# Bank order inside a group of 24 matmuls: one PSUM bank after the other instead of in turn

## What is computed

```
xn = rmsnorm(x)
u, v, q, k, va, ga, gb = split(xn @ w_in)
a  = gelu(u) * (tril(W_s) @ rmsnorm(gelu(v)) + bias)
b  = sliding_window_attention(q, k, va)
h  = sigmoid(ga) * (a @ w_oa) + sigmoid(gb) * (b @ w_ob)
x  = x + h @ w_out
x  = x + relu(rmsnorm(x) @ w_up)**2 @ w_down      # w_up 1024 x 4096
y  = rmsnorm(x)
```

## Time and profile before

| | |
|---|---|
| median of 3 runs | 1637.41 us (1636.24 to 1639.02) |
| profiled execution | 1637.21 us |
| its span, first to last instruction | 1635.5 us |
| PE busy | 1553.7 us, 95% |
| VectorE busy | 1053.4 us, 64% |
| ScalarE busy | 765.8 us, 47% |
| share of line 1538 (the matmuls of `product`) in the chain that ended last | 66.4% |
| mean granted TensorE clock | 0.977 |

### The profile page before, as it was taken

One profiled execution on the slowest core, in us unless ns is written; L12 is line 12 of the kernel. 1 busy time (PEld: TensorE's weight loads), 2 busy tenths in 40 slices (PEclk: granted clock), 3 DMA queues, 4 the chain that ended last, 5 costly groups with the idle time before them and its releaser, 6 DMA issues.

```text
span 1635.5 us, 28812 instructions
## 1 busy us (share of the span) xinstructions
PE 1553.7 (95%) x12226; PEld 1518.1 (93%) x12226; DVE 1053.4 (64%) x1377; ACT 765.8 (47%) x1159; POOL 181.7 (11%) x206
## 2 busy tenths in 40 slices
PE   3999999999998989999995999999999999999998
PEld 3988888889998989999995999999999999999997
DVE  3455554402766666766674776876687678767875
ACT  5465555522644544555441464533553355335533
POOL 4222322200000010000110040000000000000001
PEclk7999999999999999999997999999999999999999
DMA  7611110132859524545568343636363645454522
GB/s 244 195 29 27 29 29 21 35 116 78 206 162 279 156 50 106 152 107 155 130 176 218 112 115 89 170 94 165 104 155 110 149 119 140 124 135 128 132 63 104
DMA packets 105353, 200.64 MB, mean 123 GB/s; under 512 B 16592, under 2 KB 44240, under 8 KB 97896
## 3 DMA queue, kind: packets, MB, share of 16 engines
q1 hardware_dynamic: 88288, 127.64, 23.4%
q0 software_dynamic: 10384, 64.00, 20.1%
q10 hardware_dynamic: 6552, 7.13, 1.3%
HBM read 121.77 MB, written 19.30 MB: 86 GB/s over the span
## 4 chain that ended last, share of the span: by engine, by line
PE 82%; DMA 5%; DVE 5%; ACT 4%; issue 2%; SPq 2%; POOL 1%; ACTq 0%; DVEq 0%; POOLq 0%
PE ps L1538 66%; PE ps L1330 10%; PE ps L1318 2%; DMA res<-x_keep 2%; ACT prob L741 1%; PE ps L1376 1%; DVE prob L1006 1%; DMA xn<-xn_keep 1%; DMA raw<-in_w_in 1%; PE ps L1394 1%; POOL prob L559 1%; SPq L407 1%; DVE y_t L1307 1%; PE ps L1516 1%; DVE w_lo L956 1%
## 5 line engine op out<-in xcount | busy, mean ns | idle before, releaser
L1538 PE MATMUL ps<-xp_hi,wp_hi 128*128 128x258 f32 x3136 | 636.0, 284 | 23.6 <-DVE wp_lo L1110 18.9
L1538 PE MATMUL ps<-xp_lo,wp_hi 128*128 128x258 f32 x3136 | 637.0, 285 | 0.0
L1538 PE MATMUL ps<-xp_hi,wp_lo 128*128 128x258 f32 x3136 | 636.0, 285 | 0.0
L1538 PEld LDWEIGHTS ps<-xp_hi,wp_hi 128*128 128x128 f32 x3136 | 491.9, 191 | 24.7 <-DVE wp_lo L1110 19.5
L1538 PEld LDWEIGHTS ps<-xp_hi,wp_lo 128*128 128x128 f32 x3136 | 491.4, 191 | 0.0
L1538 PEld LDWEIGHTS ps<-xp_lo,wp_hi 128*128 128x128 f32 x3136 | 488.3, 191 | 0.0
L677 ACT ACTIVATE wp_hi<-wbuf 128x1024 fp32r<-128x1024 f32 x196 | 208.0, 1061 | 554.2 <-PE ps L1538 553.9
L1110 DVE TENSOR_TENSOR wp_lo<-wbuf,wp_hi 128x1024 fp32r<-128x1024 f32 x196 | 243.6, 1243 | 170.5 <-ACT wp_hi L677 170.5
L1330 PE MATMUL ps<-xn_hi,w_hi 128*128 128x344 f32 x480 | 159.7, 333 | 2.0 <-DVE q_st L986 2.0
L1330 PE MATMUL ps<-xn_lo,w_hi 128*128 128x344 f32 x480 | 155.1, 323 | 0.0
L1330 PE MATMUL ps<-xn_hi,w_lo 128*128 128x344 f32 x480 | 155.1, 323 | 0.0
(11 more groups left out here) (191 smaller groups left out, 1526.4 us busy)
## 6 DMA issues: line engine op xcount, KB each, us to landing
wbuf<-wbuf POOLq DMA_DIRECT2D x57, 1024.0 KB, 7.5
wbuf<-in_w_up SPq DMA_DIRECT2D x24, 1024.0 KB, 5.5
wbuf<-in_w_down SPq DMA_DIRECT2D x24, 1024.0 KB, 5.1
wbuf<-in_w_in SPq DMA_DIRECT2D x18, 1024.0 KB, 5.6
raw<-in_w_in SPq DMA_DIRECT2D x40, 256.0 KB, 3.4
wbuf<-in_w_ob SPq DMA_DIRECT2D x6, 1024.0 KB, 7.1
wbuf<-in_w_oa SPq DMA_DIRECT2D x6, 1024.0 KB, 5.2
wbuf<-in_w_out SPq DMA_DIRECT2D x6, 1024.0 KB, 5.4
```

Of the source, the lines that this page charges most:

```text
L1538: last = mm(ps[:, 2 * p + b, 0:HN], w[:, (2 * n + p // 2) % 2, k, p % 2 * P:(p % 2 + 1) * P], x[n % 2][:, k, b * HN:(b + 1) * HN], start=( ...
```

## The change

In `product` the loop over the two halves b moves from the innermost place to the outermost. Before, the 24 matmuls of a group alternate between the two banks, and two neighbours share their weights. After, twelve go to bank 2p and then twelve to bank 2p + 1; each weight tile is read for the first half and again twelve matmuls later for the second. The number of matmuls, weight loads and waits is the same, and so are the buffers and the flags for starting and ending an accumulation in each bank. The wait for the second part of `xp_split` stands before k = 2 of the first half, which is the 7th matmul of the group instead of the 13th. `prod_done` is still raised once, by the 24th.

```diff
-                for k in range(MH):
-                    if p == 0 and k % 2 == 0:
-                        pe.wait_ge(xp_split, 2 * n + k // 2 + 1)
-                    for m, (w, x) in enumerate(passes):
-                        for b in range(2):
+                for b in range(2):
+                    for k in range(MH):
+                        if p == 0 and b == 0 and k % 2 == 0:
+                            pe.wait_ge(xp_split, 2 * n + k // 2 + 1)
+                        for m, (w, x) in enumerate(passes):
                             last = mm(ps[:, 2 * p + b, 0:HN], w[:, (2 * n + p // 2) % 2, k, p % 2 * P:(p % 2 + 1) * P],
                                       x[n % 2][:, k, b * HN:(b + 1) * HN], start=(first and k == 0 and m == 0),
                                       stop=(k == MH - 1 and m == 2), skip_group_check=not first)
```

## The result

The changed kernel is faster: median 1626.89 us of 7 runs (1625.84 to 1632.23) against 1637.41 us of the kernel before (1634.7 to 1639.71, 7 runs), ratio 0.9942 with a 95% interval of 0.9927 to 0.9957. That is 10.5 us or 0.6% less. I had forecast no change, 1637.6 us, with a range of 1629 to 1648, and missed.

A forecast was written before the change was run, and what follows sets the result against it. PE bounds the kernel, with an unbroken run of matmuls 120.6 ns apart. Counts, reading out and distance at 0 plus 0.36 us for the wait, on 1637.21 us, gave 1637.6 us, range 1629 to 1648.

The forecast's parts named there:

- What bounds the kernel: PE, busy 95% of the span, with matmuls 120.6 ns apart from 1000 us on; 0.35 ns each makes 0.2%.
- The counts and the reading out: Matmul and weight load counts stay, and both banks are still read after the 24th matmul: 0 us each.
- The wait for the second half of x: Moved to the 7th matmul, it stops PE at g = 6 for i = 0 and i = 1: 0.07 + 0.29 us.
- the 0.36 us of the sum: Total of all forecast terms, made up of 0.07 + 0.29 us from the two new stops of PE at g = 6.
- The distance from start to start: Time between starts of neighbouring matmuls in a group, 120.5 ns before: claimed unchanged, 0 us, chance 0.48.
- bounds of +1.2 and -1.3: Limits in ns on the change per matmul, carried over from 344 and 256 columns: +11.3 us and -12.2 us in all.
- same-bank row: Profile row before the change whose matmuls stay in one bank: 344 columns at 157.5 ns, or 256 columns at 118.3 ns.
- The faster one: Rival: staying in a bank is a little cheaper, 119.2 ns a matmul, 1625.4 us in all; chance 0.27.
- the scores: Matmuls of 256 columns, each low part added onto the columns just written by the high part: 118.3 ns each.
- `bank`: Profile row with 24 matmuls of 344 columns into one bank: 157.5 ns each, 14.2 ns over their columns.
- The slower one: Rival: each matmul in a group pays the price of `bank`, 14.2 ns over its columns: 1648.9 us; chance 0.23.
- PE might drop its clock by going round the banks: Skill rule cited for the faster rival: bank cycling can leave idle spots that drop the clock; no size or own chance.

The follow-up runs named there:

- first kernel: Changed kernel's operand order, but the matmuls write the two banks in turn as in the kernel before: 1627.08 us, beside 1638.36 us for the kernel before.
- second kernel: Operand order of the kernel before, but the first twelve matmuls write one bank and the last twelve the other: 1636.82 us, beside 1638.36 us for the kernel before.
- widths kernel: In nine products all matmuls of a group read one weight tile and one moving tile, 128 to 512 columns wide; 256 columns took 113.3 or 120.0 ns.

## Why the prediction was wrong

**What bounds the kernel** was right: the long piece of line 1538 kept its 5208 matmuls, and all that was won in it came from the distance between them. So was the scale: 0.35 ns decides.

**The counts and the reading out**, both put at 0, were right. VectorE and ScalarE have the load of before, and the bank finished earlier was of no use to anyone.

**The wait for the second half of x** came out as worked out, but for its end: two short stops, both at g = 6, and no other. At g = 6, i = 0, PE's timeline after shows the stop at the 7th matmul:

```profile
953.10 0.28 PE L1538 MATMUL ps<-xp_hi,wp_lo 128*128 128x258 f32 x1
953.53 0.39 PE L1538 MATMUL ps<-xp_hi,wp_hi 128*128 128x258 f32 x1 [0.16 <-DVE xp_lo L1116]
953.76 0.28 PE L1538 MATMUL ps<-xp_lo,wp_hi 128*128 128x258 f32 x1
```

From 953.10 to 953.53 are 0.43 us instead of 0.12, a stop of 0.31 (predicted 0.32), and 0.23 follow instead of 0.12, so 0.42 in all (predicted 0.43). At i = 1:

```profile
965.13 0.28 PE L1538 MATMUL ps<-xp_hi,wp_lo 128*128 128x258 f32 x1
965.46 0.39 PE L1538 MATMUL ps<-xp_hi,wp_hi 128*128 128x258 f32 x1
965.69 0.28 PE L1538 MATMUL ps<-xp_lo,wp_hi 128*128 128x258 f32 x1
...
968.58 0.24 PE L1498 MATMUL ps<-ones,sq_acc 128*128 128x1 f32 x1 [0.69 <-issue]
```

0.21 + 0.11 = 0.32 us (predicted 0.29). I had counted this in full, since the sums follow. But before the sums PE stood idle anyway, for 1.26 us before the change and 0.69 after: the stop was taken out of that. What the sums wait for is `sq_acc` from GpSimd, a wait that my account left out. Before and after:

```profile
971.23 2.98 POOL L614 TENSOR_TENSOR sq_acc<-sq_acc,sq_tmp 128x1032 f32<-128x1032 f32 x1
```

```profile
965.80 2.67 POOL L614 TENSOR_TENSOR sq_acc<-sq_acc,sq_tmp 128x1032 f32<-128x1032 f32 x1
```

It ends at 974.21 and at 968.47, and the sums start 0.1 us later in both. From the first matmul of g = 6 to the sums it is 968.58 - 952.39 = 16.19 us after and 974.31 - 957.82 = 16.49 before, so the stops did not lengthen it. The stop at i = 0 took the place of the one two groups later, as predicted. Of the 0.36 us of the sum, the 0.29 were 0, and the other 0.07 are too small to be told apart.

**The distance from start to start** is the step that failed: "Neither row shows that a bank matters [...] I take 0." The premise was right and the conclusion did not follow. The bank indeed has no effect (first and second kernel). But the change also reorders the reads of the moving tiles, and that is worth -0.83 ns on each of 9408 matmuls, -7.8 us, while I took 0 between bounds of +1.2 and -1.3. I had named "a cost of the order itself" as what would make me wrong, but gave it neither a price nor a chance. The value lies inside the bounds; to put it in their middle was a choice without a reason. I asked of each same-bank row what it says about banks, and took its extra over the columns as a law of width. The widths kernel shows what such a row is worth: instructions that differ in nothing but their buffer take 113.3 or 120.0 ns. Neither end was a bound for another address.

**The rivals.** The faster one, 1625.4 us, came nearest to the time, but by luck, for its reason is wrong: "staying in a bank is a little cheaper". What I wrote for it was misread, too: that both same-bank rows lie on or below what 120.5 ns makes one expect. It holds for the scores, but 120.5 + 86 / 2.4 = 156.3 ns for 344 columns, and `bank` has 157.5. The slower one named a part of the truth, the second half that goes on in the same row of x, with the wrong sign: at 258 + 258 columns the orders that read so are the dearer ones. That PE might drop its clock by going round the banks did not happen: with banks in turn the first kernel has the clock at 1.00 and the full gain. The Trainium skill's rule behind it (TensorE: Matmul & The Clock Gate, A second HAM failure mode: psum-queue depth-cycling) finds no support here.

**What I had not in the sum at all** is the time at half clock. It was 2.4 us shorter in the profiled execution after than in the one before, but behind one stop it differs as much between kernels that read in one and the same order (13 to 27 matmuls at g = 1), and whether the change shortens it stays open. So of the 10.5 us between the medians 7.8 are shown to come from the order of the reads.

**What stays open of the cause.** That the sequence of moving reads and their addresses change the distance is shown: by weights held fixed, by a buffer moved by 32 bytes, by starts moved by 8 to 96 bytes. A rule that tells from the addresses which sequence is cheap was not found. The values 113.3, 120.0, 153.3, 160.0, 226.7 and 233.3 ns are 17, 18, 23, 24, 34 and 35 times the time of 16 columns (6.67 ns), which are 64 bytes of a row; that it has to do with how the row is fetched is a guess. Nor can a cost of each start by itself explain it: the old and the new order read the same 24 pieces in each group, so it depends on what was read before. How far back is open: a stream of one repeated tile kept a pace of 120.00 ns in some block products and 120.83 in others, and one of 344 columns 153.3 or 157.8, for as long as it went on.

## What to carry to other kernels

Where a stream of matmuls has no idle time and still takes more than its columns, the order and the start addresses of the moving operand are a knob of about 1%, to be found by trial: put another order or cut in each stage of one kernel and read the distances between stage starts. Where a stage has a stop in it, read whole blocks behind the stop instead; two good cuts stood in such stages here. A change named after one thing (the bank) should be read for all that it reorders. And a row of another shape bounds a cost only if what differs between the two is known not to matter; where a nanosecond decides, call the sign unknown.

## What the runs showed of the hardware

- At the full clock a matmul of 256 columns of fp32r followed by the same one, each with its own weight load, takes 113.3 or 120.0 ns in the two buffers, and one of 258 columns between 116.7 and 121.6 ns by where the row starts. The Trainium skill (TensorE: Matmul & The Clock Gate, Back-to-back issue gap) gives N / 2.4 + 2.5 ns, 109.2 ns for 256 columns, for a matmul by itself, and says that in a stream of weight loads and matmuls the loads count too and that the formula is then too high at large N (131 ns measured at 512 columns). It has no term for addresses. The measurements here lie 4 to 12 ns above the formula at 256 and 258 columns, and above it at 512 too (226.7 and 233.3 ns against 215.8).
- One stream of the same instructions on the same addresses can settle at different paces: 153.3 or 157.8 ns at 344 columns, 120.00 or 120.83 at 258.
- At half clock 258 columns take 215 ns, just their columns: the extra is gone. 128 columns take 213.3 ns there, twice their columns.
- With the moving reads in the same sequence, it changes nothing down to 0.1 ns in a group which weight tile is loaded, and whether the same one is loaded twice in a row; nor does the PSUM bank, with accumulation going on in one or changing with every matmul.
- After the short stops of PE at g = 6, at the full clock, the first matmul is followed 0.22 to 0.23 us later, not 0.12.
